# An expert stage on one Trainium2 core, its gathers and products listed by rows: value rows between the last query blocks

## The reference

```python
def token_block(xt):                      # 128 tokens
    q = (xt @ wq).reshape(128, 8, 2, 128)
    s = einsum('thcd,hckd->thck', q, sub_keys)
    top_s, top_i = top_k(s, 16)
    cand = top_s[:, :, 0, :, None] + top_s[:, :, 1, None, :]
    best_s, best_c = top_k(cand.reshape(128, 8, 256), 16)
    expert = i1 * 128 + i2                # i1, i2 picked from top_i by best_c
    w = softmax(best_s)
    act = gelu(einsum('thkd,td->thk', u[expert], xt))
    return einsum('thk,thkd->td', w * act, v[expert])
h = h + peer_ffn(rmsnorm(h, ffn_norm), wq, sub_keys, u, v)
gate = sigmoid(rmsnorm(h, ple_gate_norm) @ ple_gate_w)
h = h + (p @ ple_proj) * gate
```

## Time and profile before

| | us |
|---|---|
| median of 3 runs | 1658.65 (1657.05 to 1663.93) |
| the profiled execution | 1658.09 |
| its span in the profile | 1656.3 |
| PE, DVE, ACT, POOL busy | 1428.2, 971.4, 537.7, 511.5 |
| expert stage, first gather to last v row used | 223.6 to 937.7 |

### The profile page before, as it was taken

One profiled execution on the slowest core, in us unless ns is written; L12 is line 12 of the kernel. 1 busy time (PEld: TensorE's weight loads), 2 busy tenths in 40 slices (PEclk: granted clock), 3 DMA queues, 4 the chain that ended last, 5 costly groups with the idle time before them and its releaser, 6 DMA issues. The chain is left out here.

```text
span 1656.3 us, 17356 instructions
## 1 busy us (share of the span) xinstructions
PE 1428.2 (86%) x6624; PEld 942.7 (57%) x6624; DVE 971.4 (59%) x1758; ACT 537.7 (32%) x807; POOL 511.5 (31%) x550
## 2 busy tenths in 40 slices
PE   7999989477777777777777799999999989999998
PEld 6765668122222222222222376568999878689986
DVE  2245475666666666666544643555776365657763
ACT  3253321211111111111113235734444355434432
POOL 4000024477777777777676400000000000000000
PEclk9899999799999999999999999999999999999999
DMA  9323069899999999999999524324553545345543
GB/s 299 125 102 115 1 249 368 308 409 409 409 409 409 409 409 409 410 409 410 408 410 369 215 102 154 112 90 153 174 184 129 176 180 172 119 140 180 179 145 135
DMA packets 162578, 413.75 MB, mean 250 GB/s; under 512 B 11337, under 2 KB 57659, under 8 KB 162368
## 3 DMA queue, kind: packets, MB, share of 16 engines
q0 software_dynamic: 75632, 272.63, 42.0%
q1 hardware_dynamic: 86544, 138.58, 24.8%
q10 hardware_dynamic: 320, 1.43, 0.2%
HBM read 411.55 MB, written 1.05 MB: 249 GB/s over the span
## 5 line engine op out<-in xcount | busy, mean ns | idle before, releaser
L2219 DVE SCALAR_TENSOR_TENSOR arena<-arena,ps 128x1024 f32<-128x1024 f32 x256 | 308.5, 1220 | 209.1 <-DMA arena<-in_peer_u,routes 208.0
L2602 POOL DMA_INDIRECT arena<-in_peer_u,routes x256 | 242.9, 949 | 151.6 <-issue 63.2
L1812 DVE TENSOR_TENSOR w_lo<-ring,w_hi 128x2048 fp32r<-128x2048 f32 x66 | 151.1, 2292 | 103.0 <-ACT w_hi L1652 103.0
L1547 ACT ACTIVATE state<-cst,gatew 128x128 f32<-128x128 f32 x240 | 90.6, 397 | 349.2 <-PE ps L1047 340.6
L1652 ACT ACTIVATE w_hi<-ring 128x2048 fp32r<-128x2048 f32 x66 | 126.3, 1917 | 177.4 <-PE ps L1187 88.3
L1047 PE MATMUL ps<-mixed,state 128*128 128x512 f32 x240 | 118.4, 617 | 56.3 <-ACT state L1547 31.4
L1047 PE MATMUL ps<-wX,state 128*128 128x512 f32 x240 | 117.3, 611 | 38.6 <-ACT state L1547 20.4
L1047 PE MATMUL ps<-xT,state 128*128 128x512 f32 x240 | 117.3, 611 | 37.6 <-ACT state L1547 27.1
L1047 PE MATMUL ps<-proj,state 128*128 128x512 f32 x240 | 117.3, 611 | 37.5 <-DMA proj<-in_peer_v,routes 19.4
L1047 PEld LDWEIGHTS ps<-mixed,state 128*128 128x128 f32 x240 | 41.5, 192 | 133.1 <-ACT state L1547 73.3
L1047 PEld LDWEIGHTS ps<-wX,state 128*128 128x128 f32 x240 | 40.7, 189 | 115.2 <-issue 66.8
(11 more groups left out here) (449 smaller groups left out, 2325.7 us busy)
## 6 DMA issues: line engine op xcount, KB each, us to landing
ring<-in_ffn_w_up SPq DMA_DIRECT2D x22, 2048.0 KB, 8.8
ring<-in_ffn_w_down SPq DMA_DIRECT2D x22, 1024.0 KB, 4.8
ring<-in_even_w_in SPq DMA_DIRECT2D x7, 2048.0 KB, 7.7
ring<-in_w_in SPq DMA_DIRECT2D x6, 2048.0 KB, 10.0
ring<-in_odd_w_in SPq DMA_DIRECT2D x6, 2048.0 KB, 7.8
ring<-in_peer_wq SPq DMA_DIRECT2D x4, 2048.0 KB, 8.4
ring<-in_w_out SPq DMA_DIRECT2D x2, 2048.0 KB, 7.8
arena<-in_peer_u,routes POOLq DMA_INDIRECT x256, 12.1
```

Of the source, the lines that this page charges most:

```text
L1547: do(diags[n % DIAGS], ident, ACT.Copy, scale=gatew[:, u * UROWS + b:u * UROWS + b + 1]).then_inc(diag_ready, 1)
L1812: v.tensor_tensor(w_lo[j % 2][:], w, w_hi[j % 2][:].bitcast(F32), ALU.subtract).then_inc(lo_ready, 1)
L2219: v.scalar_tensor_tensor(row, row, 1.0, token_tile(u // PAIR_UNITS), ALU.mult, ALU.mult, accum_out=dots[:, b:b + 1]).then_inc(u_used, 1)
L2602: pool.indirect_dma_start(arena[:, b % GATHER_SLOTS, :], None, a["peer_u"][0], route_of(u, b))\
```

## The change

The expert stage's lists are written again by rows, on all four engines.

- **POOL**: v rows start after 16 u rows. `u_ahead(n)` is the number of u rows issued before v row n: 16 for rows 0 to 3, 24 for rows 4 to 7, then 25 and slowly growing to n + 24 (it was n + 33). Unit 0's v rows have slots of their own (`first_slots`: in `mixed`, the used-up half of `wX`, `proj`, `hn`, `aTm` and `reset`), so that `sk_done` is only waited for ahead of row 34. The load of `p` moves behind row 40. `aTm` and `reset` are filled anew by three memsets at the end of POOL's list, which `chunk_decays` in the last layer waits for.
- **PE**: v rows 0 to 13 stand between the blocks of `both_queries(2)` and `both_queries(3)`, whose scores go to other banks. The side input's transposes come ahead of row 48, its product ahead of rows 51 and 54 (`PLE_ROWS`).
- **ACT**: `logits_exp(0)` moves ahead of the second query copy, `head_gelu(0, 0)` and 14 diagonals ahead of the last query copies; the side input's copies and `token_copied(1)` move to rows 50 and 58; in later units the gelu of a unit's first head stands 4 rows ahead of that unit.
- **DVE**: `tile_norm(1)` comes ahead of the first product, products of unit 0 come before and between `best_keys(1, ...)`, `best_shares(0)` and `head_weights(0, 0)` stand ahead of row 16; the choosing for a unit is done one unit ahead of its products, as before two ahead of its v rows. Three of the four `mix_split` of the gate's weights move from behind rows 16, 21 and 26 of unit 7 to behind rows 19, 23 and 27.

```diff
@@ -49,14 +49,22 @@
-GATE_CAST = (9, 15, 21, 27)
+GATE_CAST = (15, 19, 23, 27)
+PLE_ROWS = (48, 51, 54)
...
+
+
+def u_ahead(n):
+
+    if n < GATHER_SLOTS:
+        return (16, 24)[n // 4]
+    return min(n + 17 + min((n - GATHER_SLOTS) // 4, 7), UNITS * UROWS)
...
@@ -323,8 +331,10 @@
-        v_slots = [mixed[:, 0, :], mixed[:, 1, :], xT_rows[:, 0, :], xT_rows[:, 1, :],
-                   wX[:, 2048:3072], wX[:, 3072:4096], proj[:, 0:1024], proj[:, 1024:2048]]
+        first_slots = [mixed[:, 0, :], mixed[:, 1, :], wX[:, 0:1024], wX[:, 1024:2048],
+                       proj[:, 6144:7168], hn[:, 0, :], aTm[:].rearrange("p a n -> p (a n)"), reset[:]]
+        later_slots = [mixed[:, 0, :], mixed[:, 1, :], xT_rows[:, 0, :], xT_rows[:, 1, :],
+                       wX[:, 2048:3072], wX[:, 3072:4096], proj[:, 0:1024], proj[:, 1024:2048]]
...
@@ -974,15 +994,33 @@
+            def value_row(n):
...
+                pe.wait_ge(diag_ready, nth + 1)
+                pe.wait_ge(v_landed[b % GATHER_SLOTS], 16 * (n // GATHER_SLOTS + 1))
+                for half_ in range(2):
+                    last = mm(ps[:, 4 + 2 * (u // PAIR_UNITS) + half_, :], diags[nth % DIAGS], v_slot(u, b)[:, 512 * half_:512 * half_ + 512],
+                              start=(u % PAIR_UNITS == b == 0),
+                              stop=(u % PAIR_UNITS == PAIR_UNITS - 1 and pe_rows_before(u, b + 1) == pe_rows_before(u, UROWS)),
+                              skip_group_check=True)
+                last.then_inc(v_pe_used, 1)
...
+                    if j == 2 * HPAIR - 1:
+                        last.then_inc(chunk_done, 1)
+                    for n in rows_after[j]:
+                        value_row(n)
...
@@ -1014,41 +1052,45 @@
-            for c, bank in ((2, 2), (3, 0)):
-                both_queries(c, bank)
+            pe.wait_ge(sk_read, UNITS // 2)
+            both_queries(2, ((), (0, 1), (2, 3), (4, 5)))
+            key_scores(2, 5)
+            key_scores(2 + PAIR_UNITS, 5)
+            value_row(6)
+            value_row(7)
+            both_queries(3, ((8, 9), (10, 11), (12,), (13,)))
+            key_scores(3, 6)
+            key_scores(3 + PAIR_UNITS, 6)
...
+            for n in range(14, UNITS * UROWS):
+                if n == PLE_ROWS[0]:
+                    ple_turned_in()
+                elif n in PLE_ROWS[1:]:
+                    ple_product(PLE_ROWS.index(n) - 1)
+                if n == PAIR_UNITS * UROWS:
                     pe.wait_ge(u_used, PAIR_UNITS * UROWS)
+                value_row(n)
...
@@ -1498,6 +1540,13 @@
...
+            logits_exp(0)
...
@@ -1505,46 +1554,51 @@
...
+            for c, rows_before in ((2, range(0, 6)), (3, range(6, 14))):
+                for n in rows_before:
+                    row_weights(n)
+                query(c, psf[:, 1024:2048])
+                for tt in range(TT):
+                    scores_out(c + PAIR_UNITS * tt)
+            logits_exp(1)
+            head_gelu(0, 1)
...
+                if n == PLE_ROWS[0] + 2:
+                    act.wait_ge(ple_turned, 1)
+                    do(pT.rearrange("p k t -> p (k t)"), ps[:, 0, :], ACT.Copy).then_inc(pleT_ready, 1)
+                if n == PLE_ROWS[-1] + 4:
+                    act.wait_ge(chunk_done, CHUNK_AT["ple_proj"] + 1)
+                    for side in (0, 1):
+                        do(ple[:, side, :], pair(side), ACT.Copy).then_inc(pair_read[side], 1)
+                    token_copied(1)
+                if b == UROWS - 4 and u + 1 < UNITS:
+                    head_gelu(u + 1, 0)
+                if b == 12 and u:
+                    head_gelu(u, 1)
+                if b == 14 and 0 < u < UNITS - 1:
+                    logits_exp(u + 1)
+                row_weights(n)
...
@@ -1836,6 +1890,7 @@
+                dve.wait_ge(rebuilt, 2)
...
@@ -2271,57 +2318,63 @@
+            tile_norm(1)
             dve.wait_ge(token_ready, 1)
-            products(0, 0, 1)
-            tile_norm(1)
-            for hd in range(HPAIR):
-                best_keys(1, hd)
+            products(0, 0, 8)
+            best_keys(1, 0)
+            products(0, 8, 8)
+            best_shares(0)
+            best_keys(1, 1)
+            head_weights(0, 0)
+            products(0, 16, 4)
...
-            products(0, 1, 7)
             places(1)
             route(1)
-            products(0, 8, 12)
-            best_shares(0)
-            products(0, 20, 8)
-            head_weights(0, 0)
-            products(0, 28, 4)
+            products(0, 20, 12)
+                more = u + 1 < UNITS
...
+                    best_keys(u + 1, 0)
+                products(u, 0, 3)
+                head_weights(u - 1, 1)
                     expert_sum(0)
                 if more:
...
-                both_rows(u, 6, 6)
+                    best_keys(u + 1, 1)
+                products(u, 5, 4)
...
+                products(u, 9, 3)
...
-                if not after_:
...
+                products(u, 12, 3)
...
+                products(u, 15, 3)
                 if more:
-                    route(u + 2)
-                if not after_:
-                    mix_split(gate + 2)
-                both_rows(u, 27, 5)
+                    route(u + 1)
+                best_shares(u)
+                products(u, 18, 2)
+                head_weights(u, 0)
+                products(u, 20, 8)
+                if more:
+                    products(u, 28, 4)
...
+            for b in range(28, UROWS):
+                products(u, b, 1)
+                if not v_on_pe(u, b - 27):
+                    weighted_row(u, b - 27)
+            for b in range(5, UROWS):
+                if b == 10:
+                    head_weights(u, 1)
+                if not v_on_pe(u, b):
+                    weighted_row(u, b)
+                if b - 4 in GATE_CAST[:-1]:
+                    mix_split(gate + GATE_CAST.index(b - 4))
...
@@ -2587,45 +2640,58 @@
...
-            pool.wait_ge(idx_ready, 1)
-            for b in range(UROWS):
-                gather_u(0, b)
-            pool.wait_ge(sk_done, UNITS)
-            for u in range(UNITS):
-                if u + 1 < UNITS:
-                    pool.wait_ge(idx_ready, u + 2)
-                for b in range(UROWS):
-                    if u + 1 < UNITS:
-                        gather_u(u + 1, b)
-                    gather_v(u, b)
+            n_u = 0
+            for n in range(UNITS * UROWS):
+                while n_u < u_ahead(n):
+                    gather_u(n_u)
+                    n_u += 1
+                if n == 0:
+                    pool.wait_ge(tile_turned, 2 * TILE_TURNS.index(("out1", 1)) + 2)
+                    pool.wait_ge(s_done, TT * NH)
+                    pool.wait_ge(pv_done, TT)
+                    pool.wait_ge(token_ready, 1)
+                    pool.wait_ge(cl_o_done, TT)
+                elif n == UROWS + 2:
+                    pool.wait_ge(sk_done, UNITS)
+                gather_v(n)
+                if n == UROWS + GATHER_SLOTS:
+                    load_p()
+            pool.memset(reset[:], 1.0).then_inc(blanked, 1)
+            pool.memset(aTm[:], 0.0).then_inc(rebuilt, 1)
+            pool.wait_ge(blanked, 1)
+            pool.memset(grid(reset[:], HH * NCH, CH)[:, :, 0], 0.0).then_inc(rebuilt, 1)
```

More of the change, by code:

```diff
@@ L1507, in _ @@
             scores_out(PAIR_UNITS + 1)
-            for c, bank in ((2, 2), (3, 0)):
-                query(c, psf[:, 512 * bank:512 * bank + 1024])
-                for tt in range(TT):
-                    scores_out(c + PAIR_UNITS * tt)
-            act.wait_ge(ple_turned, 1)
-            do(pT.rearrange("p k t -> p (k t)"), ps[:, 0, :], ACT.Copy).then_inc(pleT_ready, 1)
-            act.wait_ge(chunk_done, CHUNK_AT["ple_proj"] + 1)
-            for side in (0, 1):
-                do(ple[:, side, :], pair(side), ACT.Copy).then_inc(pair_read[side], 1)
-            token_copied(1)
-            def logits_exp(u):
-                part = slice(u * UROWS, (u + 1) * UROWS)
-                act.wait_ge(idx_ready, u + 1)
-                do(gatew[:, part], gatew[:, part], ACT.Exp).then_inc(best_exp, 1)
             def head_gelu(u, hd):
```

145 lines of the change are left out of this document (61 added, 84 removed).

## The result

The changed kernel takes 1650.64 us (median of 7 runs, 1645.10 to 1652.86), beside 1660.72 for the kernel before (7 runs in the same comparison, 1657.05 to 1663.93): a ratio of 0.994, 95% interval 0.9925 to 0.9955. The forecast was 1640.5 us with a range of 1637 to 1647, a gain of 17.6 us; the gain measured is 10.1 us, and the time lies outside that range. The sign was right, the size was not. The profiled execution of the change has a span of 1648.5 us.

The account below looks back on a forecast made before the run. The prediction took DMA at 409 GB/s as the bound, with POOL only feeding it. From the profiled 1658.09 us, -18.6 (early waits) + 0.5 (thin feeding) + 0.5 (side input) gave 1640.5 us, range 1637 to 1647.

Parts of the forecast that it names:

- DMA is the bound, POOL feeds it: Expert stage: DMA at 409 GB/s sets the pace, 1.28 us a row; only stretches where DMA is not full can shorten.
- The early waits, -18.6 + 0.5: 240 to 320 us: the DMA shortfall of 18.6 us goes; 0.5 us is lost to thin feeding at row 14.
- The split between the two parts: Opening, POOL's two waits: 280 to 310 us holds 12.0 of the 18.6; the second wait is for unit 0's exp.
- Side input, 0.5: Side input's transposes and product, now inside the v rows: the queue covers PE's lateness; cost 0.5 us, bounds 0 and 5.3.
- Unit edges, 0: Edges between units: u rows 24 ahead of v rows instead of 33 cost 0 us.
- Memsets, 0: Three memsets at POOL's end: nobody waits for POOL then; cost 0 us, bounds 0 and 2.1.
- Tail, "I take 0": End of stage: 23 v rows without a u row beside them keep the same pace, moved `mix_split` cancel out; 0 us.
- PE's pace in the opening: Rival, up to row 14: row 0's weights come 10 us late and PE sets the pace; about 1649 us, chance 0.12.
- POOL's issue as the bound: Rival, expert stage: POOL's lost issues count, not DMA's shortfall; 26 us gained, 1632 us, chance 0.04.
- DVE's choosing: Rival of no change, from 242 us on: DVE's choosing pieces stop POOL, some 33 us; about 1655 us, chance 0.05.
- the unit edges: Rival of slower, 7 edges: late weights or indices stop POOL, unhidden cost 29 us; 1670 us, chance 0.06.

Follow-up runs that it names:

- e7: The kernel before with 16 diagonals instead of 8 and nothing else changed: 1660.81 us, ratio 0.9998 to the kernel before.
- e10: The kernel before with only the exp of unit 0 moved ahead in ACT's list, and 16 diagonals: 1650.53 us, ratio 0.9934 to the kernel before.
- e8: The changed kernel with 16 diagonals instead of 8: 1651.21 us, ratio 0.9936 to the kernel before.
- e9: The changed kernel with 16 diagonals and DVE's value rows three rows earlier in its list: 1646.52 us, ratio 0.9905 to the kernel before.
- e5: The changed kernel again, unaltered, on a chip with stops: 1718.34 us beside 1739.64 for the kernel before, ratio 0.9876.

## Why the prediction was right in sign and wrong in size

- *DMA is the bound, POOL feeds it.* Held. The shortfall against 409 GB/s gives the stage's gain to within some 2 us: 13.5 by shortfall and 13.0 measured for the change; and against e7, about 11 and 10.8 for e10, 11.5 and 9.2 for e8, 17 and 14.7 for e9.
- *The early waits, -18.6 + 0.5.* Held: 0.6 is left at 240 to 320 and 0.2 at 320 to 340. The first diagonal was to come at 262 and row 0 started on PE at 261.9; v row 8 was to go out at 267 and went at 270.3; row 14 was to be through at 322 and was at 323.5; u row 28 was to wait about 5 us until 281 and waited 4.98 until 283.7. DVE's wait for the second head's gelu, forecast at some 10 us, was 6.3.
- *The split between the two parts.* The text said that 280 to 310 holds 12.0 of the 18.6 and that the second wait is for the exp. e10 takes 11.5 to 12.1 away with the exp alone.
- *Side input, 0.5.* Held: 407 GB/s from 400 to 450 us, 0.2 us. *Unit edges, 0.* Held: 409 from 450 to 860. *Memsets, 0.* Held: they run from 919.1 to 921.1, before the last row at 923.7.
- *Tail, "I take 0".* **This step failed.** It was +4.0 us of shortfall in the first profile and +5.5 in e8 against e7, and e9, which only moves DVE's rows, has the 5.5 back. The text counted the value rows without a u row beside them, and POOL's slowed gathers, and took their pace as given. It did not ask who frees the slots. With 24 rows of lead the first value rows of the last unit land while u rows are still to come; DVE, which takes half of them, works its list in order, and the change puts row (7,1) behind product 28. POOL is at row (7,9) 8 us before the u row of product 28 is in. A count like that of the opening, made from the earlier trace rows, would have shown this stop, but at less than half its size. Eight issues behind u row 28 POOL is at row (7,9), 9.9 us later; with a landing of 12.1 us, a product of 1.2 and DVE's row of 1.3 the slot comes free at 14.6, a stop of 4.7 us (an estimate), which the 7 us of queue would have seemed to cover. u row 28 took 18.2 us to be used, not 12.1, and that makes the 10.95. So a second figure of the text was off: it carried the 12.1 us of the earlier trace rows over to the changed kernel. The median there is 17.3; it is 17.2 in e9 as well, but 11.6 in e7 and 12.6 in e10, so the deeper queue comes with the new order. The Trainium skill (Perfetto Trace Analysis, "Tensor Engine Instruction") says that ACT, DVE and GpSimd are strict FIFOs; the trace agrees, with row (7,1) landed at 871.1 and taken at 881.25. One reading of the text is not shown: it says that the trace does not agree with the rule that it gives from the Trainium skill (SBUF — State Buffer, "Who interferes with whom"). But a gather also reads its indices, `routes`, and no run tells whether that or the writing of descriptors is what took 1.90 instead of 0.94 us.
- *The size of the whole.* Forecast 17.6; with the tail as it was in the two profiles, 12 to 13.6; measured 10.1 and 10.2. Against the profile from which the forecast was made, the stage gained 13.0 of the 17.6 us, and the rest of the program took 4.9 us longer. The forecast was made against a profile of 1658.09, whose rest of 719.9 us is the shortest of 20 profiles (719.9 to 728.6, median 724.0) of one and the same code; e7 and e10, which have the kernel before but for the diagonals and the exp, have 723.9 and 727.0. So nothing says that the 4.9 us which the change seemed to lose after the stage are its own: about half of the distance between 1640.5 and the time measured is the luck of that one profile, and not the tail. With the stop mended (e9) the gain is 14.8 of the 17.6; of the other 2.8, what makes them is open.
- *Rivals.* PE's pace in the opening, POOL's issue as the bound, DVE's choosing, the unit edges: none came. By the time alone one would have taken the first, which gives about 1649 us; but its sign, a dip under 380 GB/s at 310 to 340, is absent, with 405 there. No stretch of 550 us went over 409 GB/s, and the edges show no dip. The rival that would have been needed, an order of DVE that holds a slot at the end, was not among them.

## What to carry to other kernels

Where an in-order engine both consumes rows and frees slots, count both ends of the stage with the same care: for each slot that comes up, when its row landed and when the engine's list lets it be taken. Before a large change of order, try its cheapest part alone: here one line of ACT's list brought as much as all of it. Compare the stage and not the span between two profiles, since code that nobody touched varied by 8.7 us. And a landing time that is mostly queue can't be carried over to a kernel that keeps the queue fuller.

## What the runs showed of the hardware

- A chip can show stops that another has not: on four chips ACT stood before its diagonals with no releaser in the trace (e5: 236 us in 53 waits within 520 us, the longest 13.6), and POOL too (e5: up to 4.9 us), and DMA moved 368 to 374 GB/s instead of 409 through the whole middle of the stage. Their cause is open; 16 diagonals did not change it. The same change was worth 10 us on the one kind and 21 on the other.
- The landing of a gather is queue for the most part: the row issued at 853.00 landed after 18.1 us, that issued at 882.80, after POOL's stop, after 7.3. At the same 409 GB/s the median was 12.1 us in one order of the rows and 17.3 in the other.
- A PE that had stood 3.17 us did its next row in 3.75 instead of 1.96 us; the granted clock of that 10 us window was 0.64.
